# Scan masks times dt on ScalarE in place of GpSimd, and a new order for Silu, skipped input and transposed result

## The reference, cut to what matters

```python
acs = jnp.cumsum(da, axis=-1)
seg = acs[..., :, None] - acs[..., None, :]
lmat = jnp.where(lower, jnp.exp(jnp.where(lower, seg, 0.0)), 0.0)
cb = jnp.einsum('bclgn,bcsgn->bcgls', cc, bc)
y_diag = jnp.einsum('bcgls,bcgrls,bcsgrp->bclgrp', cb, lmat, xdt)   # xdt = x * dt
```

## Time and profile before

| | |
|---|---|
| median of 3 runs | 3046.21 us (3046.17 to 3049.14) |
| the profiled execution, its own time | 3040.79 us |
| its span, first to last instruction | 3038.7 us |
| mean granted TensorE clock | 0.866 |
| PE, DVE, ACT, POOL busy | 77%, 72%, 42%, 42% of the span |
| the scans of the 8 groups | about 620 to 1150 us of the span |

### The profile page before, as it was taken

One profiled execution on the slowest core, in us unless ns is written; L12 is line 12 of the kernel. 1 busy time (PEld: TensorE's weight loads), 2 busy tenths in 40 slices (PEclk: granted clock), 3 DMA queues, 4 the chain that ended last, 5 costly groups with the idle time before them and its releaser, 6 DMA issues.

```text
span 3038.7 us, 38874 instructions
## 1 busy us (share of the span) xinstructions
PE 2331.5 (77%) x15054; PEld 2052.7 (68%) x15054; DVE 2201.6 (72%) x2801; ACT 1266.4 (42%) x2063; POOL 1288.7 (42%) x825
## 2 busy tenths in 40 slices
PE   6899999999999999999999870000233329999997
PEld 2578889988888888999997870000132328888886
DVE  1434446877788873444554599999999989999997
ACT  1233334545555464333334320000598924434433
POOL 0000000245555630000000567667688856767763
PEclk8899999999999999999999985555555559999999
DMA  9887876544454459976554359999999978999996
GB/s 403 335 305 290 294 292 213 183 151 160 154 176 156 153 175 347 350 256 246 194 194 179 126 221 421 403 365 354 408 421 421 422 283 297 366 367 370 367 381 233
DMA packets 152794, 868.47 MB, mean 286 GB/s; under 512 B 18865, under 2 KB 31169, under 8 KB 74705
## 3 DMA queue, kind: packets, MB, share of 16 engines
q1 hardware_dynamic: 68578, 449.03, 39.6%
q0 software_dynamic: 73872, 406.08, 34.5%
q10 hardware_dynamic: 10160, 10.88, 1.0%
HBM read 836.81 MB, written 27.39 MB: 284 GB/s over the span
## 4 chain that ended last, share of the span: by engine, by line
PE 46%; DVE 24%; DMA 9%; issue 9%; POOL 8%; ACT 3%; DVEq 0%; ACTq 0%; SPq 0%; POOLq 0%
PE bank L1792 29%; DVE u_ring L1651 8%; POOL u_ring L736 8%; PE bank L1778 7%; PE bank L2192 4%; DMA v_got<-in_v_rest,expert 4%; DMA raw<-in_tiles 3%; DVE w_lo L1197 3%; PE bank L1817 2%; DVE peer_g L1692 2%; DVE conv L1311 1%; DMA u_ring<-in_peer_u,expert 1%; DVE c_lo L1705 1%; DMA v_raw<-in_v_dense 1%; DVE y_w L1369 1%
## 5 line engine op out<-in xcount | busy, mean ns | idle before, releaser
L1197 DVE TENSOR_TENSOR w_lo<-raw,w_hi 128x1024 fp32r<-128x1024 f32 x450 | 600.2, 1347 | 544.5 <-ACT w_hi L781 540.3
L781 ACT ACTIVATE w_hi<-raw 128x1024 fp32r<-128x1024 f32 x482 | 501.2, 1058 | 638.1 <-PE bank L1792 340.9
L1792 PE MATMUL bank<-h_lo,w_hi 128*128 128x256 f32 x2048 | 591.2, 289 | 13.3 <-DVE h_lo L1243 8.7
L1792 PE MATMUL bank<-h_hi,w_lo 128*128 128x256 f32 x2048 | 580.4, 283 | 0.0
L1792 PE MATMUL bank<-h_hi,w_hi 128*128 128x256 f32 x2048 | 580.3, 283 | 0.0
L736 POOL DMA_INDIRECT u_ring<-in_peer_u,expert x256 | 509.2, 1989 | 165.7 <-DVE act_p L1651 80.0
L1651 DVE CUSTOM_DVE_ANT_0 u_ring<-u_ring,h_t 128x2048 f32<-128x2048 f32 x192 | 430.7, 2287 | 9.2 <-DMA u_ring<-in_peer_u,expert 7.9
L743 POOL DMA_INDIRECT v_got<-in_v_rest,expert x256 | 359.2, 1403 | 177.7 <-DVE peer_g L1692 133.7
L1792 PEld LDWEIGHTS bank<-h_lo,w_hi 128*128 128x128 f32 x2048 | 393.6, 192 | 56.1 <-issue 24.9
L1792 PEld LDWEIGHTS bank<-h_hi,w_lo 128*128 128x128 f32 x2048 | 393.8, 192 | 0.9
L1792 PEld LDWEIGHTS bank<-h_hi,w_hi 128*128 128x128 f32 x2048 | 393.4, 192 | 0.0
(11 more groups left out here) (317 smaller groups left out, 4832.3 us busy)
## 6 DMA issues: line engine op xcount, KB each, us to landing
raw<-in_tiles SPq DMA_DIRECT2D x337, 1024.0 KB, 5.4
v_raw<-in_v_dense SPq DMA_DIRECT2D x128, 660.0 KB
s_t<-in_states POOLq DMA_DIRECT2D x8, 512.0 KB, 7.1
y_hi_rows<-y_hi_e POOLq DMA_DIRECT2D x16, 256.0 KB, 2.4
y_lo_rows<-y_lo_e POOLq DMA_DIRECT2D x16, 256.0 KB, 6.3
gate_rows<-gate_buf ACTq DMA_DIRECT2D x8, 512.0 KB, 5.3
y_hi<-y_hi_rows POOLq DMA_DIRECT2D x8, 512.0 KB, 8.0
y_lo<-y_lo_rows POOLq DMA_DIRECT2D x8, 512.0 KB, 3.9
```

The lines of the kernel that those rows point to most:

```text
L781: act.activation(w_hi[:, i % RING], raw[:, slot % SLOTS, (n % 2) * 2 * CH:(n % 2 + 1) * 2 * CH], ACT.Copy) \
L1197: dve.tensor_tensor(w_lo[:, i % RING], raw[:, n // 2 % SLOTS, (n % 2) * 2 * CH:(n % 2 + 1) * 2 * CH], w_hi[:, i % RING].bitcast(F32), ALU. ...
L1792: ins = pe.matmul(spot if x.shape[1] == KT else spot.rearrange("p (s t) -> p s t", s=NS), w[:, col], moving, start=start and k == 0 and m ...
```

## The change

The two products of `dt_masked` go from POOL to ACT: 8 instructions of 128x128 each (one per head, dt as a per-partition scale) instead of one of 128x1024. POOL keeps the sum. ACT does the two products of (g,1) at t=7 and 8, those of (w,0), the next group, at t=12 and 13. The Silu of xs moves from t=15 to 14, ahead of `norm(g,1)`; `result_hi(g,0)` moves from t=13 to 15. On DVE `skipped(g,1)` moves from t=10 to 12, behind `mix(g,1)`, and `result_lo(g,0)` from 13 to 15. On PE `turn_result(g,0)` moves from t=12 to 14, behind `products(g,1)`. Two semaphores of later stages (`g1_bc`, `g2_bc`) become one, `gain_bc`, which makes room for the new `ssd_dt`.

```diff
 POOL, dt_masked(g, s)
-                if u:
-                    pool.wait_ge(ssd_mix, u)
-                pool.tensor_tensor(dt_mix[:], up_eq[:].unsqueeze(1).broadcast_to([P, HPG, P]), per_head(dt_t, s, 0, g),
-                                   ALU.mult).then_inc(ssd_dm, 1)
-                pool.tensor_tensor(dt_low[:], low_eq[:].unsqueeze(1).broadcast_to([P, HPG, P]), per_head(dt_t, s, 1, g),
-                                   ALU.mult).then_inc(ssd_dm, 1)
-                pool.wait_ge(ssd_dm, 3 * u + 2)
+                pool.wait_ge(ssd_dt, 2 * u + 2)
                 pool.tensor_tensor(dt_mix[:], dt_mix[:], dt_low[:], ALU.add).then_inc(ssd_dm, 1)
 ACT
+            def dt_masked(g, s, d):
+                u = 2 * g + s
+                if u == 0 and d == 0:
+                    act.wait_ge(dt_ready, 4)
+                    act.wait_ge(dt_exp, 4)
+                if u:
+                    act.wait_ge(ssd_mix, u)
+                    act.wait_ge(ssd_dm, u)
+                for h in range(HPG):
+                    col = g * HPG + h
+                    ins = act.activation((dt_mix, dt_low)[d][:, h], (up_eq, low_eq)[d][:], ACT.Copy,
+                                         scale=dt_t[:, s, d, col:col + 1])
+                ins.then_inc(ssd_dt, 1)
...
                         decays(g, 1)
+                        dt_masked(g, 1, 0)
+                    elif t == 8:
+                        dt_masked(g, 1, 1)
...
-                    elif t == 13:
+                    elif t == 15:
                         result_hi(g, 0)
-                    elif t == 15:
                         norm(g, 1)
-                if t == 15 and w < GROUPS:
+                if t in (12, 13) and w < GROUPS:
+                    dt_masked(w, 0, t - 12)
+                if t == 14 and w < GROUPS:
                     conv_act(4 + w, conv[:])
 DVE
-                    dve.wait_ge(ssd_dm, 3 * u + 3)
+                    dve.wait_ge(ssd_dm, u + 1)
...
-                    elif t == 10:
-                        skipped(g, 1)
                     elif t == 11:
                         mix(g, 1, 0)
                         mix(g, 1, 1)
-                    elif t == 13:
-                        result_lo(g, 0)
+                    elif t == 12:
+                        skipped(g, 1)
                     elif t == 14:
                         combine(g, 1)
+                    elif t == 15:
+                        result_lo(g, 0)
 PE
-                elif t == 12:
-                    turn_result(g, 0)
                 elif t == 13:
                     products(g, 1)
+                elif t == 14:
+                    turn_result(g, 0)
```

More of the change, by code:

```diff
@@ L412, in program @@
         ssd_dm = sem("ssd_dm")
+        ssd_dt = sem("ssd_dt")
         mask_r = sem("mask_r")
@@ L440, in program @@
         g1_in = sem("g1_in")
-        g1_bc = sem("g1_bc")
+        gain_bc = sem("gain_bc")
         g1_copied = sem("g1_copied")
@@ L476, in program @@
         g2_in = sem("g2_in")
-        g2_bc = sem("g2_bc")
         g2_copied = sem("g2_copied")
@@ L1026, in side @@
                     if h == 3:
-                        act.wait_ge(g1_bc, j + 1)
+                        act.wait_ge(gain_bc, j + 1)
                         if j >= 2:
@@ L1174, in _ @@
                     n = (i - 68) // 2
-                    act.wait_ge(g2_bc, n + 1)
+                    act.wait_ge(gain_bc, 4 + n + 1)
                     act.activation(g2_b[:, n // 4, (n % 4) * CH:(n % 4 + 1) * CH], psum[6 + n % 2][:], ACT.Copy) \
@@ L1997, in spread_g1 @@
                     ins = pe.matmul(psum[4 + s][:], comb_b[:, s], g_rows[:, j * CH:(j + 1) * CH], start=True, stop=True)
-                ins.then_inc(g1_bc, 1)
+                ins.then_inc(gain_bc, 1)
             def key_scores(j):
@@ L2201, in _ @@
                     pe.matmul(psum[6 + n % 2][:], comb_b[:, n // 4], g2_rows[:, (n % 4) * CH:(n % 4 + 1) * CH],
-                              start=True, stop=True).then_inc(g2_bc, 1)
+                              start=True, stop=True).then_inc(gain_bc, 1)
 OUTPUTS = [("y_prompt", (1, P, D)), ("y_sample", (1, P, D)),
```

## The result

The changed kernel takes 3031.62 us (3029.17 to 3034.46, 4 runs) where the kernel before takes 3047.68 (3046.17 to 3049.78, 4 runs): a ratio of 0.9948, 95% interval 0.9933 to 0.9963. That is 16 us faster, under half of the 36 us of the forecast, though 3031.6 lies inside its range.

A forecast was written before the change was run, and what follows sets the result against it. PE was taken as close to the bound, stalled by late DVE and ACT, with DVE slowed beside POOL. Seven transitions times 5.1 us gave 36 us off 3046.2, so 3010 us; range 2991 to 3033.

The forecast's parts named there:

- Masks off POOL: DVE beside a silent POOL: two `xdec` and the skipped input take 2.0 us instead of 7.5.
- `mix(g,1)` and `products(g,1)`: DVE and PE: `mix(g,1)` ends at 804.0, 5.4 us earlier; `products(g,1)` waits 1.1 us for it at full clock.
- The stall before `turn_result(g,0)`: PE's wait for the normalised result: 2.85 us, plus 3.0 us of slow clock per window, both gone.
- ACT's chain from there: ACT from the end of `mix(g,1)` at 804.0 through calls, splits, Silus and norm to the split of half 3' at 823.1.
- The added table load: ACT, before the Silu of z behind the norm's Exp: 1.28 us more, without the skill's drain of about 1.38.
- The last collision: `w_lo` of half 3' on DVE meets POOL's `masked(g+1,1)`, takes 2.4 us; PE waits 1.8 us, until 825.5.
- the main sum: Whole scan: window 61.3 us against 66.3 to 66.5, 7 transitions times 5.1 = 36 us, giving 3010 us.
- The merged semaphores and the order of the last window: Later stages and the last window, where PE has no stall on the scan: costed at nothing.
- Rival 2: The clock still falls on PE's small waits, 3.0 us per window: 7 x 2.1 = 15 us gained, 3031 us; chance 0.18.
- Rival 1: All stalls go and PE alone sets the pace: window 58.9 us, 53 us gained, 2993 us; chance 0.20.
- Rival 3: ACT becomes the bound: copies over 0.64 us each lose the gain; at 0.8, 18 us slower, 3064 us; chance 0.07.
- Rival 4: Collisions with POOL only move between 787 and 804, so `mix(g,1)` ends where it did: 3046 us; chance 0.05.

The follow-up runs named there:

- e4: Changed kernel with the two Silus of z on ACT moved behind the split of half 3' of the next group's xs: 3034.10 us, ratio 0.9949.
- e10: Kernel before with the masks moved to ACT and, of the new order, only `skipped(g,1)` behind `mix(g,1)` on DVE: 3018.13 us, ratio 0.9905.
- e5: Changed kernel with POOL's `masked(g,1)` started ahead of both saves of y instead of behind one: 3009.58 us, ratio 0.9876.
- e9: Changed kernel with POOL's `masked` cut to one head of eight from the third chunk on: 2986.26 us, ratio 0.9798.
- e11: Changed kernel with POOL's `masked(g,1)` waiting until DVE has done `w_lo` of half 4 of the next window's first kind: 2996.88 us, ratio 0.9847.
- e8: Changed kernel with the eight scaled copies of each ACT call issued a second time: 3107.40 us, ratio 1.0206.
- e12: Changed kernel with the diffs of both e11 and e4: 3008.08 us, ratio 0.9885.
- e2: Kernel before with the new order on ACT, DVE and PE, the masks staying on POOL: 3056.79 us, ratio 1.0038.
- e1: Changed kernel with the masks on ACT but the order of before on ACT, DVE and PE: 3032.41 us, ratio 0.9952.

## Why the prediction was right in its direction and wrong in its size

**Masks off POOL: right.** DVE's products in the shadow of POOL, kernel after (start, us):

```profile
779.75 1.29 DVE L1373 TENSOR_TENSOR xdec<-xs_t,e_acs 128x512 f32<-128x512 f32 x2
780.95 0.69 DVE L1381 TENSOR_TENSOR y_w<-xs_t,dt_par 128x512 f32<-128x512 f32 x1
```

1.98 in place of 7.5, predicted 2.0. ACT's call, predicted 2.5, takes 2.45, in the grouping and in the window:

```profile
779.67 2.45 ACT L858 ACTIVATE dt_mix<-up_eq,dt_t 128x128 f32<-128x128 f32 x8
```

POOL's 75 us less and ACT's 80 more came out as 89 and 82.5.

**`mix(g,1)` and `products(g,1)`: right.** Times in the window of after are 1.53 behind those of before (784.13 for `products(g,0)` against 785.66). `products(g,1)` started at 801.88 + 1.53 = 803.4, predicted 804.0, with a wait of 0.36 against 1.1, and at full clock. (Half 13 would have ended at 803.05 by the text's own terms, 800.3 and 2.75, and not at 802.9; nothing hangs on it.) The stall before `turn_result(g,0)` and its slow clock are gone, as said.

**ACT's chain from there: right.** `xs_turned` began at 817.85 + 1.53 = 819.4, which puts half 2' 0.8 earlier than in the text (820.6 less the transposes' 0.4). `w_hi` of half 3' let `w_lo` start at 820.67 + 1.53 = 822.2, 0.9 before the 823.1 of the text. The added table load is 1.28, with nothing behind it:

```profile
817.32 1.28 ACT L1015 ACT_TABLE_LOAD   x1
818.61 1.08 ACT L1015 ACTIVATE z_g<-bank 128x512 f32<-128x512 f32 x2
```

Load and Silu are 0.01 us apart (817.32 + 1.28 = 818.60), and the instruction before the load ends 0.02 ahead of it (816.58 + 0.72 = 817.30). The drain that the Trainium skill (ScalarE: Activation LUTs, What ACT_TABLE_LOAD costs) puts on a switch does not show in these rows; the measurement decides. It would not have mattered: e4 takes the load and the Silu from ahead of the split and the time stays.

**The last collision: wrong, and it is the step that failed.** The text had `w_lo` of half 3' meet `masked(g+1,1)` and take 2.4, as a `w_lo` beside POOL had taken 2.80: one POOL product of waiting at most. It took 3.96, because it was not let in between two of POOL's products. Half 3' started at 824.69 + 1.53 = 826.2 in place of 825.5, though PE was ready 0.9 earlier than thought (826.2 - 3.4 = 822.8, against 823.7): a wait of 3.4 in place of 1.8. And the text let the clock stay up through it; it fell and cost 2.9. The sum of the window, predicted and measured: 5.1 less 0.7 (half 3' later) less 2.9 is 1.5, and 66.4 - 64.9 is 1.5. So of the 3.6 us that the forecast had too much per window, 2.9 is the clock, which the main sum put at nothing, and 0.7 the longer `w_lo`.

A wait of 1.8 would not have kept the clock up for certain either. The text took that from the one stall of 1.71 in its window. The kernel before has four stalls of 1.71 there (in the other transitions PE waits 0.3 at `xs_turned`), and behind the first, at 692.89, the clock fell:

```profile
694.00:696.00 2.00, 2.00 (x12) 0.50 0.00 0
```

In e10 it fell behind four of seven stalls of 1.7, in e5 behind three of seven waits of 2.0.

The remaining gain is at the start. From the first `products` to the last group's first one the seven periods shrank by 14.1 us: the six steady ones by 1.5 each, 9.1 in all, and the first one by 5.0 (719.35 - 650.6 = 68.8 before, 719.19 - 655.4 = 63.8 after). In that first one, from 655 to 720 us, PE waited 6.4 us before (2.8, 1.7, 1.3 and 0.6) and 3.8 after (3.4 and 0.4), and the clock fell twice before (0.50 in the 2 us from 670 and from 694) and once after (from 698). That is most of the 5.0; the forecast took its window to be like the others. The merged semaphores and the order of the last window, costed at nothing, were not tried by themselves; 14.2 us of the 16.1 lie in the scans, which leaves 2 for all else.

**Rivals.** Rival 2, that the clock still falls, gave 3031, which is what was measured, and its mechanism is the one seen, a fall of 3.0 once per window. But the number agrees partly by luck: it had the wait itself at 1.8 and left out the larger gain of the first period, two errors of 3 to 4 us that cancel (six windows at 0.6 less each, the first at 2.9 more). Rival 1, no stalls, 58.9 us a window, is what e9 shows when `masked` is taken away (57.9) and what e11 nearly reaches (59.75). Rival 3, ACT as the bound, did not happen at 0.31 us a copy, so copies of 0.64 were not seen. e8 doubles the calls: the text counted two of the four on the path, by which 5 us per window more would just use up its gain of 5.1, and 10.8 came. Rival 4 was near the truth in words, that the collisions only move: what moved was the one of `masked`, not that of the masks of dt.

What would have told it blind: before, `masked(g+1,1)` starts at 821.87, released by `segments`, and four products of 1.89 end at 829.4. PE starts half 3' at 830.47, 1.1 us later, after it had stalled for 1.71 at `xs_turned`. Whoever costs that stall as a gain has to let `masked` keep its 7.5 us and ask what stands over it then. The text did place `masked` at 818.4 to 826 (it ran from 816.09 + 1.53 = 817.6 to 825.1), but took the cost of the meeting from the mildest rows.

## What to carry to other kernels

A stall that a change removes may be the cover of another engine's run: before counting it as gained, look at what ran beside it (here POOL's 7.5 us of `masked`) and which instruction that PE needs at once falls into that run afterwards. When DVE and POOL collide, let POOL wait for the DVE instruction that matters, so that its run starts behind it: e11 does that in two lines, and change and wait together gain three times what the change does. The place has to be found again when the queue shifts (e12, 11 us slower). A wait of PE of 1.7 us or more should be costed both with and without a slow clock behind it, 2.9 us here.

## What the runs showed of the hardware

- **Who gets in between two POOL products.** A `w_lo` that starts while POOL is in a product, with POOL's next one ready, either goes in at the first boundary, and POOL's next product takes 2.87 in place of 1.89 (in the changed kernel `w_lo` of 2.21 from 786.76, and these POOL rows), or it is passed over to the end of POOL's run: 3.96 in the changed kernel and 6.36 in e4.

```profile
787.86 2.87 POOL L627 TENSOR_TENSOR m_hi<-up_eq,da_hi 128x1024 fp32r<-128x1024 f32 x1
```

In the two cases passed over DVE had been idle for 6.0 and 3.6 us before (their rows); in the one let in it came from `convolve` without a pause. Idle time alone is not the cause. In the kernel before a `w_lo` that follows 7.73 us of idle goes in at the first boundary, and POOL's next product takes 2.88:

```profile
762.62 1.25 DVE L1197 TENSOR_TENSOR w_lo<-raw,w_hi 128x1024 fp32r<-128x1024 f32 x1 [7.73 <-ACT w_hi L781]
```
```profile
762.75 2.88 POOL L627 TENSOR_TENSOR m_lo<-low_eq,da_lo 128x1024 fp32r<-128x1024 f32 x1
```

It starts 1.73 us into a product, those passed over 0.87 (changed kernel) and 0.33 (e4). In e2, after the same 5.75 of idle, a `w_lo` that starts 0.60 into a product takes 4.23 and one at 1.84 takes 1.22. So what decides seems to be idle time and the place in the product together; no run varied either alone, and it stays open.
- **The clock at short waits.** Waits of 3.4 us (changed kernel), 3.04 (e1) and 2.85 (before) were followed by a granted clock of 0.50 in all seven windows each, waits of 0.64 (e11) in none. In between it is either: 2.46 in e12 two of seven, 2.0 in e5 three of seven, 1.7 in e10 four of seven, 1.71 before one of four. Nor does a wait of 3 us always lower it: in e8 waits of 2.99 (at 695.80) and 3.39 (at 703.17) left it at 1.00 (2 us from 696 and from 704). What decides stays open.
- **Back-to-back copies on ACT.** Eight of 128x128 take 2.45 us, 0.31 each, and 16 take 4.93; the mean length of one is 0.39, as each overlaps the next. The price per copy does not rise with their number.
